# Recurrent block of a hybrid layer: 32x32 inverses by column elimination on GpSimd in place of four matmul levels

## The reference, cut to what matters

```
q = l2norm(q) * (DK ** -0.5); k = l2norm(k)          # l2norm(x) = x * rsqrt(sum(x*x) + EPS)
decay = exp(where(tril, G[..., :, None] - G[..., None, :], -inf))     # G = cumsum(g)
L = where(strict, einsum('bnhid,bnhjd->bnhij', k * beta, k) * decay, 0)
u, w = solve(eye + L, [v * beta, k * beta * exp(G)])                  # lower triangular
A_qk = einsum('bnhid,bnhjd->bnhij', q, k) * decay
# scan over chunks: v_new = u - w @ S;  o = q_dec @ S + A @ v_new;  S = S * exp(G_last) + k_dec.T @ v_new
o = o * rsqrt(mean(o*o) + EPS) * norm_g;  o = o * silu(z)
```

## Time and profile before

| what | value |
|---|---|
| median of 3 runs | 1493.7 us (1493.62 to 1494.52) |
| the profiled execution, its own time | 1496.4 us |
| its span | 1494.6 us |
| PE busy | 1448.2 us, 97% of the span |
| DVE busy | 822.1 us, 55% |
| ACT busy | 565.2 us, 38% |
| POOL busy | 184.7 us, 12% |

### The profile page before, as it was taken

The page is one execution under the profiler, slowest core; times in us unless marked ns, Lnnn a source line. Parts: engine busy times, 40 slices in busy tenths (PEclk is TensorE's granted clock), DMA queues, the critical chain, the costliest instruction groups (busy, mean ns, idle before and its releaser), DMA issues.

```text
span 1494.6 us, 20211 instructions
## 1 busy us (share of the span) xinstructions
PE 1448.2 (97%) x7191; PEld 1183.2 (79%) x7191; DVE 822.1 (55%) x1399; ACT 565.2 (38%) x879; POOL 184.7 (12%) x257
## 2 busy tenths in 40 slices
PE   6899999999999999999989999999998899999998
PEld 4788888888888888888867888888886667777776
DVE  4556464646465555434436665346554688954532
ACT  4424242423434242222324443234444545545432
POOL 2101010101001010000032000000014153232300
PEclk8999999999999999999999999999999999999999
DMA  4222222222222221333322332333224222222211
GB/s 145 57 57 71 57 70 56 56 56 70 56 56 70 56 56 56 85 93 104 99 85 67 93 94 84 99 113 98 82 80 119 59 55 59 57 58 70 57 57 71
DMA packets 208501, 111.46 MB, mean 75 GB/s; under 512 B 6826, under 2 KB 206793, under 8 KB 208457
## 3 DMA queue, kind: packets, MB, share of 16 engines
q1 hardware_dynamic: 208073, 110.86, 26.2%
q0 software_dynamic: 384, 0.03, 0.0%
HBM read 108.75 MB, written 2.10 MB: 74 GB/s over the span
## 4 chain that ended last, share of the span: by engine, by line
PE 88%; DVE 8%; ACT 2%; issue 1%; POOL 0%; DMA 0%; DVEq 0%; ACTq 0%; POOLq 0%
PE gb L574 66%; PE gd L700 3%; PE gd L697 2%; PE gd L688 2%; PE gd L915 2%; PE gb L966 1%; PE gd L966 1%; PE gd L894 1%; DVE selb L1708 1%; DVE small L1707 1%; DVE act_a L1348 1%; PE gd L905 1%; DVE selb L1697 1%; PE gd L586 1%; PE gd L660 1%
## 5 line engine op out<-in xcount | busy, mean ns | idle before, releaser
L574 PE MATMUL gb<-act_a,whi 128*128 128x512 f32 x2800 | 974.9, 406 | 9.1 <-ACT act_a L989 4.5
L574 PEld LDWEIGHTS gb<-act_a,whi 128*128 128x128 f32 x2800 | 527.0, 189 | 127.1 <-DVE act_a L1348 10.8
L574 PE MATMUL gb<-act_a,wlo 128*128 128x512 f32 x1488 | 581.4, 391 | 0.0
L574 PEld LDWEIGHTS gb<-act_a,wlo 128*128 128x128 f32 x1488 | 281.7, 189 | 55.2 <-issue 4.1
L981 ACT ACTIVATE whi<-raw 128x1024 fp32r<-128x1024 f32 x212 | 223.0, 1052 | 226.7 <-PE gb L574 196.9
L1319 DVE TENSOR_TENSOR wlo<-raw,whi 128x1024 fp32r<-128x1024 f32 x190 | 233.4, 1229 | 129.3 <-ACT whi L981 128.9
L574 PE MATMUL gb<-act_b,whi 128*128 128x512 f32 x304 | 109.2, 389 | 0.0
L1954 POOL TENSOR_TENSOR wlo<-raw,whi 128x1024 fp32r<-128x1024 f32 x22 | 52.7, 2397 | 145.8 <-ACT whi L981 145.8
L574 PEld LDWEIGHTS gb<-act_b,whi 128*128 128x128 f32 x304 | 57.1, 188 | 11.9
L1862 POOL TENSOR_TENSOR rr<-ss,eps_head 128x4 f32<-128x4 f32 x8 | 1.6, 201 | 493.0 <-DVE ss L1476 493.0
L688 PEld LDWEIGHTS gd<-Ti,LT 128*128 128x128 f32 x384 | 50.2, 191 | 3.9
(11 more groups left out here) (401 smaller groups left out, 1603.9 us busy)
## 6 DMA issues: line engine op xcount, KB each, us to landing
raw<-in_w_in_dram SPq DMA_DIRECT2D x103, 512.0 KB, 3.6
raw<-in_w_up_dram SPq DMA_DIRECT2D x44, 512.0 KB, 3.7
raw<-in_w_down_dram SPq DMA_DIRECT2D x16, 384.0 KB, 3.2
raw<-in_w_down_dram SPq DMA_DIRECT2D x16, 320.0 KB, 3.0
raw<-in_w_a_out_dram SPq DMA_DIRECT2D x8, 512.0 KB, 3.5
raw<-in_w_b_out_dram SPq DMA_DIRECT2D x8, 512.0 KB, 3.5
raw<-in_w_o_dram SPq DMA_DIRECT2D x8, 512.0 KB, 3.5
raw<-in_w_out_dram SPq DMA_DIRECT2D x8, 512.0 KB, 3.4
```

Source lines behind the costliest of these rows:

```text
L574: ins = pe.matmul(gb[:, b, :], l, r, start=(first and m == 0), stop=(last and m == len(todo) - 1))
```

## The change

Keys and queries are no longer scaled and transposed back: SiLU writes them straight to `KT` and `QT`, and the inverse squared key length is folded into beta (`rr[R_B2]`), into the scale of the state update (`R_BKD`), and the key length into the values (`R_KLEN`); the query length goes into the output norm. The four smallest levels (blocks of 2 to 16) are gone. In their place stands an elimination, column by column, of all sixteen 32x32 diagonal blocks at once: DVE copies row m of every block to all its partitions (`stream_shuffle`, 31 of them over steps 4 to 13, into whatever tile is free: `row_at(m)`), and POOL does, for m = 0 to 30, one multiplication and one subtraction on 4x(31-m) elements per partition of `Up`, each waiting for the one before it. DVE at step 14 waits for the last of them (`el_done`), transposes the 32x32 blocks, and spreads them into `Ui` and `Ti`; levels 4 and 5 stay as matmuls in steps 15 to 18. Key times key and the spread of the decay move to step 0 on PE, the transposition of the queries to step 4, that of the values (step 33) from unit 7 to unit 5.

```diff
 # PE
             def step(g, h):
                 if g == 0:
                     pe.wait_ge(hc_ready, h + 1)
...
+                    pe.wait_ge(conv_silu, 3 * h + 2)
+                    for c in range(TC):
+                        ins = pe.transpose(gd[:, 0, c * P:c * P + P], KT[:, c, :], ident[:])
+                    ins.then_inc(kq_turned, 1)
+                    for c in range(TC):
+                        ins = pe.matmul(gd[:, 1, c * P:c * P + P], KT[:, c, :], KT[:, c, :], start=True, stop=True)
+                    ins.then_inc(kk_done, 1)
...
-                elif g == 6:
-                    pe.wait_ge(u_ready, 7 * h + 1)
...
-                elif 7 <= g <= 18 and g % 2:
+                elif 15 <= g <= 18 and g % 2:
                     l = (g - 7) // 2
-                    if l == 0:
+                    if l == 4:
                         pe.wait_ge(t_first, h + 1)
+                        pe.wait_ge(lts_ready, h + 1)
+                        pe.wait_ge(kt_ready, h + 1)
 # ACT
             def step(g, h):
                 if g == 0:
+                    sc.wait_ge(kq_turned, 2 * h + 1)
+                    sc.activation(Ti[:], bank(gd[:, 0, :]), ACT.Square).then_inc(sq_ready, 1)
+                elif g == 1:
                     sc.wait_ge(arg_ready, h + 1)
                     sc.activation(dec[:], dec[:], ACT.Exp).then_inc(dec_ready, 1)
...
-                        if m == 3 and s > 0 and s != 3:
+                        if m == 3 and s > 1 and s != 3:
                             second_half(h, s - 1)
+                        if m == 1 and s == 2:
+                            second_half(h, 0)
 # DVE
+            def shuffles(g, h):
+                if g == 4:
+                    dve.wait_ge(lp_ready, h + 1)
+                    dve.tensor_copy(Up[:], idp[:].unsqueeze(1).to_broadcast([P, TC, B]))
+                if 4 <= g <= 13:
+                    for m in range((g - 4) * (B - 1) // 10, (g - 3) * (B - 1) // 10):
+                        dve.stream_shuffle(row_at(m), Lp[:, :, m + 1:B], [m] * B).then_inc(sh_ready, 1)
...
+                elif g == 2:
                     dve.wait_ge(kk_done, 2 * h + 1)
-                    dve.wait_ge(decb_ready, h + 1)
...
+                    dve.wait_ge(dec_ready, h + 1)
+                    dve.tensor_tensor(LT[:], bank(gd[:, 1, :]), dec[:], ALU.mult).then_inc(lt_ready, 1)
+                elif g == 3:
                     dve.wait_ge(lt_ready, 2 * h + 1)
+                    dve.wait_ge(b2_ready, h + 1)
+                    for b in range(P // B):
+                        r = slice(b * B, b * B + B)
+                        ins = dve.tensor_tensor(Lp[r, :, :], LT[r, :, b * B:b * B + B],
+                                                rr[r, R_B2, :].unsqueeze(2).to_broadcast([B, TC, B]), ALU.mult)
+                    ins.then_inc(lp_ready, 1)
...
+                elif g == 14:
+                    dve.wait_ge(el_done, (B - 1) * h + (B - 1))
+                    dve.transpose(Tp[:].rearrange("p c i -> p (c i)"),
+                                  Up[:].rearrange("p c i -> p (c i)")).then_inc(tp_ready, 1)
+                    dve.tensor_tensor(blocked(Ui), spread(Up), mask4, ALU.mult)
+                    dve.wait_ge(tp_ready, h + 1)
+                    dve.tensor_tensor(blocked(Ti), spread(Tp), mask4, ALU.mult).then_inc(t_first, 1)
 # POOL
             def head_a(h):
                 pool.wait_ge(ss_ready, 2 * h + 1)
...
+                pool.wait_ge(klen_ready, h + 1)
+                for m in range(B - 1):
+                    n = B - 1 - m
+                    pool.wait_ge(sh_ready, (B - 1) * h + m + 1)
+                    pool.tensor_tensor(elt[:, :, 0:n], row_at(m), Up[:, :, m:m + 1].to_broadcast([P, TC, n]),
+                                       ALU.mult).then_inc(el_used, 1)
+                    pool.wait_ge(el_used, (B - 1) * h + m + 1)
+                    pool.tensor_tensor(Up[:, :, m + 1:B], Up[:, :, m + 1:B], elt[:, :, 0:n],
+                                       ALU.subtract).then_inc(el_done, 1)
+                    pool.wait_ge(el_done, (B - 1) * h + m + 1)
```

More of the change, by code:

```diff
@@ L74, with row_places @@
 W_ORDER = (5, 6, 7, 2, 3, 4, 0, 1)
+B = 32
+def row_places():
+    left = [T] * TC
+    out = []
+    for m in range(B - 1):
+        n = TC * (B - 1 - m)
+        t = next(i for i in range(TC) if left[i] >= n)
+        out.append((t, T - left[t]))
+        left[t] -= n
+    return out
+ROWS = row_places()
+R_B2, R_KLEN, R_BKD = 3, 0, 7
 MASKED = -3.0e38
@@ L631, in step @@
                 if g == 0:
[L633 to L640, removed]
                     pe.wait_ge(hc_ready, h + 1)
@@ L1080, in second_half @@
                     sc.wait_ge(conv_done, 3 * h + s + 1)
-                    dst = (qc, kc, vc)[s]
-                    sc.activation(dst[:], dst[:], ACT.Silu).then_inc(conv_silu, 1)
+                    if s == 0 and not (isinstance(h, int) and h == 0):
+                        sc.wait_ge(ks_done, 3 * h)
+                    src = (qc, kc, vc)[s]
+                    dst = (flat(QT), flat(KT), vc[:])[s]
+                    sc.activation(dst, src[:], ACT.Silu).then_inc(conv_silu, 1)
                 elif s == 5:
@@ L1110, in head @@
                             second_half(h, 2)
-                        if s == 7 and m == 2:
+                        if s == 5 and m == 2:
                             step(33, h)
@@ L1437, in step @@
-                    dve.tensor_tensor(Ui[:], Ui[:], over(ident[:]), ALU.add).then_inc(u_ready, 1)
-                    dve.wait_ge(kk_done, 2 * h + 2)
-                    dve.tensor_tensor(AT[:], bank(gd[:, 3, :]), dec[:], ALU.mult).then_inc(lt_ready, 1)
-                elif 7 <= g <= 18 and g % 2:
+                    dve.wait_ge(b2_ready, h + 1)
[3 more added lines that the diff above has]
+                                                rr[r, R_B2, :].unsqueeze(2).to_broadcast([B, TC, B]), ALU.mult)
@@ new lines, in step @@
+                    ins.then_inc(lp_ready, 1)
+                elif 4 <= g <= 13:
+                    if g == 5:
+                        dve.wait_ge(kk_done, 2 * h + 2)
+                        dve.tensor_tensor(AT[:], bank(gd[:, 3, :]), dec[:], ALU.mult).then_inc(lt_ready, 1)
+                    elif g == 6:
+                        dve.wait_ge(sq_ready, 2 * h + 2)
+                        dve.tensor_reduce(ss[:, 1, :], ob[:], AX_X, ALU.add).then_inc(ss_ready, 1)
+                elif g == 14:
[5 more added lines that the diff above has]
+                    dve.tensor_tensor(blocked(Ti), spread(Tp), mask4, ALU.mult).then_inc(t_first, 1)
+                elif 15 <= g <= 18 and g % 2:
@@ L1536, in head @@
                     for m in range(4):
+                        if s >= 3:
+                            shuffles((s - 3) * 4 + m, h)
                         if late and m == 1:
@@ L1557, in _ @@
             with dve.Fori(1, HEADS) as h:
-                own.enter(h - 1, 11)
+                own.enter(h - 1, 9)
                 head(h, False)
@@ L1834, in _ @@
             pool.memset(negT[:], 0.0)
-            pool.memset(mhalf[:], -0.5)
+            link(pool.memset(blk[:], 0.0))
+            for b in range(P // B):
+                r = slice(b * B, b * B + B)
+                link(pool.tensor_copy(idp[r, :], ident[r, b * B:b * B + B]))
             pool.memset(eps_one[:], EPS)
-            link(pool.memset(eps_head[:], P * EPS))
+            pool.memset(eps_head[:], P * P * EPS)
+            link(pool.memset(mhalf[:], -0.5))
             keep(triu[:], ones[:], [[1, P]], 0, -1)
```

161 lines of the change are left out of this document (84 added, 77 removed).

## The result

The changed kernel takes 1550.93 us (median of 4 runs, 1549.49 to 1551.48) against 1494.11 for the kernel before in the same comparison (4 runs, 1493.62 to 1496.35): a ratio of 1.0369, 95% interval 1.0357 to 1.0382. The span of the profiled execution grew from 1494.6 to 1549.6 us, by 55.0. The forecast was 1554, range 1512 to 1600.

What follows compares the result with a forecast made beforehand. PE, busy 97% of the span, was taken to bound the kernel. Removed work -94, wait for `hc` +13, idle for `Ti` +130 and clock +12 gave +61 us, so 1554 us against the median, range 1512 to 1600.

Steps and rivals of the forecast that it cites:

- (d): The forecast case: elimination on POOL takes 27 to 36 us per head, time 1525 to 1597 us, chance 0.70.
- idle time for `Ti`: PE stands at the first level matmul until the elimination's result is there: 16.2 us per head, 130 us in all.
- the loss by the clock: PE runs partly at the lower clock behind each stall: 1.5 us per head, 12 us in all.
- PE work removed: Level matmuls, transpositions and changes of work taken off PE: 11.8 us per head, 94 us over eight heads.
- wait for `hc`: PE stalls at step 0 for DVE's late copy of `hc`: 1.9 us in heads 1 to 7, 13 us.
- start of the elimination after PE's slot: POOL can begin the elimination 10.6 us after PE reaches step 0.
- length of the elimination: POOL's 62 instructions with handoffs and waiting for DVE: 30.7 us per head.
- held up by DVE: In the elimination POOL loses about the length of every DVE operation with two SBUF inputs: 5.1 us per head.
- second handoff: Register instruction carrying the wait between a subtraction and the next multiplication on POOL: 0.04 us, 31 times, 1.2 us.
- rival (c): POOL is disturbed by every DVE operation, shuffles too, or handoffs cost twice: 1605 us and above, chance 0.1.
- (b): POOL is not disturbed by DVE: elimination 24.4 to 27 us, time 1492 to 1525 us, chance 0.14.
- (a): The elimination is hidden behind PE's work and the gain stays; it must be below 23 us; chance 0.06.

Runs made afterwards that it cites:

- experiment 2: Changed kernel with `hc` copied earlier on DVE, no longer behind POOL's norm of the head before: 1536.5 us, ratio 1.027 to the kernel before.
- experiment 4: Changed kernel with the weight splits of units 5 to 7 replaced by equally long sums reading one SBUF tile: 1533.26 us, ratio 1.0251 to the kernel before.
- experiment 5: Changed kernel with the elimination on 16x16 blocks (15 columns, not 31) and one more matmul level: 1482.59 us, ratio 0.9916 to the kernel before.
- experiment 3: Changed kernel with 60 useless matmuls on PE ahead of the wait for `Ti`: 1536.1 us, ratio 1.0277 to the kernel before.
- experiments 5 and 9: The 9: kernel of experiment 5 with `hc` copied early and DVE's two-input work moved out of the elimination: 1449.92 us, ratio 0.9685 to the kernel before.

## Why the prediction was right, point by point

The mechanism was (d): PE stands for `Ti`, because the elimination on POOL is longer than PE's work ahead of it. That the sum came out within 4 us is in part luck. The idle time for `Ti` was put 11 us too high over the eight heads and the loss by the clock 11 us too low, and the two cancel. The terms compare with the trace as follows (per head, us):

| term | forecast | measured | read from |
|---|---|---|---|
| PE work removed | 11.8 | 12.1 | step 0 to the level of step 15: 36.88 before, 25.24 now without the wait; 0.44 behind it |
| wait for `hc` | 1.9 | 1.7 | waits of PE |
| start of the elimination after PE's slot | 10.6 | 11.3 | 360.97 to 372.23 |
| length of the elimination | 30.7 | 29.4 | 372.23 to 401.59 |
| of it held up by DVE | 5.1 | 3.2 | five long instructions, against the forecast's prices |
| of it second handoff | 1.2 | 2.4 | 0.16 against 0.08, 30 times |
| PE at the first level | 27.0 | 26.9 | 360.97 to 387.90 |
| behind the elimination on DVE | 1.9 | 1.6 | 401.59 to 403.16 |
| idle for `Ti` | 16.2 | 14.9 (15.3 in heads 1 to 7) | waits of PE: 119.1 / 8 |
| behind the stall, mostly the clock | 1.5 | 2.9 (2.2 of it shown to be clock) | below |

**The saving.** Over eight heads 97 us instead of 94, right.

**The wait for `hc`.** 12.2 us instead of 13, and experiment 2 showed that it adds to the other and is not swallowed by it.

**The elimination.** Prices by element and the fixed 0.19 us held (the 62 instructions without what held them up: 19.0 us, 19.4 by the forecast's prices): 0.46 us for 124 elements in the subtraction, 0.40 in the multiplication with its spread operand, 0.21 for 4. Two smaller terms were off and cancelled in part. The handoff from a subtraction to the next multiplication is the full two steps (0.16 us in the brackets above), 2.4 us and not the 1.2 of the middle. That DVE holds POOL up was right, but an operation of DVE does not cost POOL its whole length: POOL lost what was left of the split when its instruction started, less about 0.15 us. That was 0.8 us per split here (1.17 instead of 0.40, and 2.4 / 3 in experiment 4) and not 1.1; in experiment 5, where the instruction started 0.03 us into a split, it was 1.05. In all it came to 3.2 us: 0.77 + 0.79 + 0.85 for the splits, and 0.8 for the two filter steps, from instructions of 0.77 and 0.71 us in place of 0.3. The scaling, which the forecast had in its 5.1 (the parts that it lists give 5.3), cost next to nothing in this head: 0.36 us for the 88 elements beside it, 0.34 by the prices. The shuffles (0.16 to 0.29 us each) cost POOL nothing, and of rival (c) only its other half came in part, the double handoff, at 1.2 us more than forecast and not 6. 3.2 us held up puts out (b), and experiment 4 shows what holds POOL up. At 29.4 us the elimination is far above the 23 that (a) needed.

**The clock.** This was the term that I mis-sized. From the end of the wait for `Ti` to PE's next spread of the decay it took 36.77 us in the mean of seven heads (35.64 to 38.5). The same work in the earlier trace rows took 32.59, of which the transposition of the values, 0.44, now stands earlier; 32.15, and 1.70 for `hc`. That leaves 2.9 us per head, 23 us in all and not 12. Filling the stall (experiment 3) gave back 2.2 of it per head, so that much is the clock's, 17 us in all; in the 0.7 that stay PE waits 0.44 us for DVE's mask `Yb` behind the first group:

```profile
400.13 1.10 PE L728 MATMUL gd<-Yb,Ui 128*128 128x64 f32 x8 [0.44 <-DVE Yb L1506]
```

The trace of before offered only a stretch of seven matmuls at the lower level behind an idle time, 3.1 us; here that level held for 4 to 10 us behind the stall. The Trainium skill (TensorE: Matmul & The Clock Gate, Part 1) has two clock levels and the lower one for an engine that has been idle; the window of 0.50 and the stall of 15.27 us ahead of it agree, and the size is from the rows here.

**The sum.** -97 + 12 + 119 + 23 = +57, and the span grew by 55.0. By heads, from one first large level matmul to the next: seven times 77.28 instead of 69.41 gives 55.1; the way to the first of them is 4.2 us shorter (94.31 instead of 98.50 us; before, PE waited 2.73 there for `kc`), which I had not looked at, and the tail behind the last one 4.1 longer (914.3 instead of 910.2).

**What stays open.** What is lost behind the stall differs between the heads of the changed kernel (1.8 to 4.7 us). In experiment 2, without the wait for `hc`, it does not (2.2 to 2.5), so that wait costs clock too; how, no run here tells, nor why in experiments 5 and 9 every second head was less affected. Of the 20 us by which experiment 5 missed its forecast, 11 are not accounted for one by one.

## What to carry to other kernels

Work moved from a saturated engine to an idle one gains only if the chain there is shorter than what the saturated engine has to do meanwhile; count the chain by instruction (fixed cost plus handoff, here 0.19 + 0.12 us on POOL, 62 times), not by elements, and choose the block size at which the chain fits: 32 lost 57 us, 16 with its surroundings cleared gained 45, and 58 with the rest of the stall filled. Add to every stall of PE the clock that it loses behind it (2.2 us behind one of 15 here), and before shortening a stall at great cost, try filling it. Look at which two-input operations of DVE fall into a POOL chain that is on the path, and move them out of it.

## What the runs showed of the hardware that was not expected

PE was granted half its clock for 4 to 10 us behind a stall of 15.3 us, although it was fully busy from the stall's end (window 0.50), and experiment 5 shows the same start (1.72 us for the first group) behind 4.05 us of idle time. Useless matmuls in such a gap made the kernel faster: 60 of them by 14.8 us, 8 of them by 13.3. A POOL instruction met by a 1.24 us DVE split lost 0.77 to 0.85 us; one on 16 elements was stretched to 1.27. In POOL's loop 0.16 us lie between two dependent instructions where the wait stands on a register instruction between them, and 0.08 where it stands on the instruction itself; that the register instruction is the cause was not tested.
